# Grid attention: probabilities divided on VectorE ahead of their turn, in place of a spread of the reciprocals by transpositions

## What is computed

```python
def neighborhood_attn(q, k, v, rpb):
    ...
    def one(r):
        ...
        s = jnp.einsum('bqhd,bikhd->bhqik', qblk, kblk).astype(jnp.float32) * scale + bias
        s = jnp.where(colmask[:, None, :], s, -jnp.inf)
        p = jax.nn.softmax(s.reshape(B, H, GRID_W, kr * GRID_W), axis=-1)
        ...
        return jnp.einsum('bhqik,bikhd->bqhd', p, vblk)
...
            y = jnp.concatenate([yc, ym], axis=-1) * jax.nn.silu(gate)
            x = x + y @ w_out_odd[o]
```

## Time and profile before

| | |
|---|---|
| median of 3 runs | 2340.4 us (2339.95 to 2343.82) |
| profiled execution, time | 2340.63 us |
| profiled execution, span from first to last instruction | 2338.9 us |
| TensorE busy | 2257.0 us (96% of the span) |
| VectorE busy | 1584.3 us (68%) |
| ScalarE busy | 1305.0 us (56%) |
| GpSimd busy | 683.1 us (29%) |
| chain of work that ended last | TensorE 81%, VectorE 9%, ScalarE 4% |
| grid attention stage | about 1025 to 1545 us |

### The profile page before, as it was taken

The page is one execution under the profiler, slowest core; times in us unless marked ns, Lnnn a source line. Parts: engine busy times, 40 slices in busy tenths (PEclk is TensorE's granted clock), DMA queues, the critical chain, the costliest instruction groups (busy, mean ns, idle before and its releaser), DMA issues.

```text
span 2338.9 us, 35387 instructions
## 1 busy us (share of the span) xinstructions
PE 2257.0 (96%) x11778; PEld 1918.3 (82%) x11778; DVE 1584.3 (68%) x3262; ACT 1305.0 (56%) x3054; POOL 683.1 (29%) x843
## 2 busy tenths in 40 slices
PE   7999999999999999999999999899999999999999
PEld 6888888888888878888888888787787888887887
DVE  7444677677886433346655566658888878889787
ACT  6444566666775444446565566655656645465542
POOL 3455232311235642222222222565563200000000
PEclk9999999999999999999999999999999999999999
DMA  7322101111233342322322322633343633345734
GB/s 229 116 76 60 41 28 37 32 35 48 62 121 109 99 136 68 95 68 86 95 85 80 95 87 88 193 91 117 100 145 108 202 96 95 109 151 167 231 116 137
DMA packets 332356, 241.69 MB, mean 103 GB/s; under 512 B 66448, under 2 KB 284816, under 8 KB 331664
## 3 DMA queue, kind: packets, MB, share of 16 engines
q1 hardware_dynamic: 332176, 239.43, 33.6%
HBM read 195.59 MB, written 43.78 MB: 102 GB/s over the span
## 4 chain that ended last, share of the span: by engine, by line
PE 81%; DVE 9%; ACT 4%; issue 3%; DMA 1%; POOL 1%; SPq 1%; DVEq 0%; ACTq 0%; POOLq 0%
PE PS L1943 15%; PE PS L1945 15%; PE PS L1944 15%; PE PS L2176 6%; PE PS L2177 6%; PE PS L2178 6%; PE PS L2092 5%; PE PS L2059 5%; PE PS L2045 2%; PE PS L2046 2%; ACT PY L2187 1%; PE PS L2101 1%; PE PS L2000 1%; DVE ST L2555 1%; PE PS L2083 1%
## 5 line engine op out<-in xcount | busy, mean ns | idle before, releaser
L2852 POOL TENSOR_TENSOR WS<-WR,WS 128x256 fp32r<-128x256 f32 x635 | 493.4, 798 | 990.9 <-ACT WS L2187 990.1
L1943 PE MATMUL PS<-HT,WS 128*128 128x512 f32 x1492 | 602.5, 404 | 18.2 <-POOL WS L2852 6.2
L1945 PE MATMUL PS<-HT,WS 128*128 128x512 f32 x1492 | 584.0, 391 | 0.0
L1944 PE MATMUL PS<-HT,WS 128*128 128x512 f32 x1492 | 582.3, 390 | 0.0
L1943 PEld LDWEIGHTS PS<-HT,WS 128*128 128x128 f32 x1492 | 281.2, 188 | 76.6 <-issue 12.2
L1945 PEld LDWEIGHTS PS<-HT,WS 128*128 128x128 f32 x1492 | 280.7, 188 | 61.6
L1944 PEld LDWEIGHTS PS<-HT,WS 128*128 128x128 f32 x1492 | 281.7, 189 | 52.0
L2187 ACT ACTIVATE WS<-WR 128x256 fp32r<-128x256 f32 x658 | 245.3, 410 | 90.1 <-PE PS L1945 57.7
L2187 ACT ACTIVATE PT<-PS 128x512 fp32r<-128x512 f32 x352 | 186.2, 529 | 193.5 <-PE PS L2059 192.9
L2445 DVE TENSOR_TENSOR PT<-PS,PT 128x512 fp32r<-128x512 f32 x352 | 211.1, 609 | 84.5 <-ACT PT L2187 81.5
L2092 PE MATMUL PS<-PT,QKV 128*128 128x256 f32 (+3 forms) x1248 | 207.8, 288 | 3.5 <-DVE YB L2624 2.4
(11 more groups left out here) (284 smaller groups left out, 4554.9 us busy)
## 6 DMA issues: line engine op xcount, KB each, us to landing
WR<-in_w_in_odd SPq DMA_DIRECT2D x106, 256.0 KB, 2.9
EO<-in_grid SPq DMA_DIRECT2D x48, 384.0 KB, 3.1
WR<-in_ffn_in SPq DMA_DIRECT2D x60, 256.0 KB, 2.9
WR<-in_w_in_even SPq DMA_DIRECT2D x100, 128.0 KB, 2.5
WR<-in_w_out_odd SPq DMA_DIRECT2D x48, 256.0 KB, 2.8
yd<-PY SPq DMA_DIRECT2D x44, 256.0 KB, 3.3
EO<-in_ffn_in SPq DMA_DIRECT2D x35, 256.0 KB, 3.1
WR<-in_w_in_even SPq DMA_DIRECT2D x34, 256.0 KB, 2.9
```

Of the source, the lines that this page charges most:

```text
L1943: e.matmul(out, wh, rh, start=start, stop=False)
L1944: e.matmul(out, wh, rl, start=False, stop=False)
L1945: return e.matmul(out, wl, rh, start=False, stop=stop)
L2852: e.tensor_tensor(ws(i, 1, n), RAW[raw_slot(u)][:, o:o + n], f32(ws(i, 0, n)), ALU.subtract).then_inc(s_wlop.sem, 1)
```

## The change

For chunks of the kinds in `EARLY`, here grid attention alone, the softmax is divided before the turn. A new step "divide" multiplies each probability tile in `PY` by its column of reciprocals and by 0.5 on VectorE, in place. The reciprocals are made just before it, and the turn waits for it (`s_div`). The finish of such a chunk has no transpositions of `RW`, no copy into `RW`, and no multiplication of the gate by the spread reciprocals. In `stream`, the reciprocals and divisions of the waiting job are put ahead of the new job's scores; in `drain`, ahead of `begin_job`. Memory attention and the even layer are as before.

```diff
+EARLY = ("c",)
...
+        self.early = kind in EARLY
...
-        self.y = fin + (2 if c.mem else 4)
+        self.y = fin + (2 if c.mem else 4) - c.early
...
-            s.wide = s.x == 1 and s.h == 1
+            s.wide = s.x == 1 and s.h == 1 and not s.c.early
...
+        def divide(job):
+
+            for s in job.scores:
+                recip(s)
+            for s in job.scores:
+                s.divided = s_div.add()
+                put("divide", s)
...
-            f = Fin(c, pp, s_spread.add(), s_fin.n, s_yc.n, s_pv.n, c.rec[pp])
-            s_fin.add(2 if c.mem else 4)
+            f = Fin(c, pp, s_spread.n if c.early else s_spread.add(), s_fin.n, s_yc.n, s_pv.n, c.rec[pp])
+            s_fin.add(f.y - f.fin)
...
-            if job:
+            if job and not job.c.early:
                 for s in job.scores:
                     recip(s)
...
+            if job.c.early:
+                divide(job)
             begin_job(job)
...
                     job = pend["job"]
+                    if job and job.c.early:
+                        divide(job)
                     s0 = score(c, pp, h, 0)
...
                     w.wait_ge(s_exp, job.scores[1].no)
+                    if job.c.early:
+                        w.wait_ge(s_div, job.scores[1].divided)
                     w.wait_ge(*until[B_PT + pb])
...
                     f, = of
+                    if f.c.early:
+                        until[B_O] = (s_fin, f.y if f.c.mem else f.fin + 2)
+                        continue
                     w.wait_ge(s_rec, f.rec)
...
+                elif kind == "divide":
+                    s, = of
+                    p, rd = p_at(s.c, s.slot, 0, s.nk), RD[:, s.pp % 2, s.x, s.h:s.h + 1]
+                    w.wait_ge(s_rec, s.rec)
+                    e.tensor_scalar(p, p, rd, 0.5, ALU.mult, ALU.mult).then_inc(s_div.sem, 1)
...
-                    w.wait_ge(s_spread, f.no)
                     w.wait_ge(s_ed, max(c.gate) if c.grid else c.gate[f.pp // 2])
-                    e.scalar_tensor_tensor(out=sg, in0=spread, scalar=0.5, in1=sg, op0=ALU.mult, op1=ALU.mult).then_inc(s_fin.sem, 1)
+                    if not c.early:
+                        w.wait_ge(s_spread, f.no)
+                        e.scalar_tensor_tensor(out=sg, in0=spread, scalar=0.5, in1=sg, op0=ALU.mult, op1=ALU.mult).then_inc(s_fin.sem, 1)
```

More of the change, by code:

```diff
@@ L345, in build @@
         s_mm, s_ea, s_ed, s_flip, s_rs, s_rp = (signal(n) for n in ("s_mm", "s_ea", "s_ed", "s_flip", "s_rs", "s_rp"))
-        s_score, s_mx, s_exp, s_sink, s_rec = (signal(n) for n in ("s_score", "s_mx", "s_exp", "s_sink", "s_rec"))
+        s_score, s_mx, s_exp, s_sink, s_rec, s_div = (signal(n) for n in ("s_score", "s_mx", "s_exp", "s_sink", "s_rec", "s_div"))
         s_turn, s_pth, s_ptl, s_pv = (signal(n) for n in ("s_turn", "s_pth", "s_ptl", "s_pv"))
@@ L2613, in vector_program @@
                             w.wait_ge(sig, value)
-                    w.wait_ge(s_spread, f.no)
                     w.wait_ge(s_ed, max(c.gate) if c.grid else c.gate[f.pp // 2])
-                    e.scalar_tensor_tensor(out=sg, in0=spread, scalar=0.5, in1=sg, op0=ALU.mult, op1=ALU.mult).then_inc(s_fin.sem, 1)
+                    if not c.early:
+                        w.wait_ge(s_spread, f.no)
+                        e.scalar_tensor_tensor(out=sg, in0=spread, scalar=0.5, in1=sg, op0=ALU.mult, op1=ALU.mult).then_inc(s_fin.sem, 1)
                     if c.mem:
                         w.wait_ge(s_pv, f.pv)
-                        w.wait_ge(s_fin, f.fin + 1)
+                        w.wait_ge(s_fin, f.y - 1)
                         e.tensor_tensor(y, PS[:, B_O, 0:256], sg, ALU.mult).then_inc(s_fin.sem, 1)
@@ L2624, in vector_program @@
                         e.tensor_tensor(YB[HALF[x], :], YB[HALF[x], :], PS[HALF[x], B_O, 256 * x:256 * x + 256], ALU.add).then_inc(s_fin.sem, 1)
-                    w.wait_ge(s_fin, f.fin + 3)
+                    w.wait_ge(s_fin, f.y - 1)
                     e.tensor_tensor(y, yb, sg, ALU.mult).then_inc(s_fin.sem, 1)
```

## The result

The changed kernel takes 2502.7 us in the median of four runs (2497.2 to 2505.7), against 2342.1 for the kernel before, measured beside it. The ratio is 1.0683, with a 95% interval of 1.0660 to 1.0707: 6.8% slower. The forecast was 2487 us (6% more), with 2440 to 2535 as the range.

The account below looks back on a forecast made before the run. TensorE was taken to bound the grid stage. From 2340.6 us, less 7.7 for transpositions, plus 124 of waits and 30 of lower clock, the forecast was 2487 us, range 2440 to 2535.

Parts of the forecast that it names:

- What bounds the kernel, and the place: Grid stage: TensorE bounds, busy 508.41 of 520 us; VectorE's multiplications behind the projection's low halves delay the turn.
- The transpositions, -7.7 us: Grid finishes on TensorE: 64 transpositions go, worth 0.12 us each from start to start, 7.7 us less.
- The price behind the table add's old start, 1.0 us: Each grid job: two reciprocals, two multiplications and hand-over make probabilities ready 1.0 us after the table add's old start.
- The waits, 124 us net: TensorE's turns in the grid stage: waits for VectorE recur in every job and add up to 124 us.
- The clock, 30 us: TensorE in the grid stage: 19 falls to half clock after waits, 1.6 us each, 30 us.
- Outside the stage, nothing: Ahead of and behind the grid stage: nothing changes except the place of what follows.
- Rival 1: Grid stage: waits come but the clock holds, or waits are partly swallowed; 2457 down to 2435 us; chance 0.20.
- Rival 2: Grid stage: half clock follows nearly every wait, 75 us; 2532 us, or 2549 with dearer multiplications; chance 0.15.
- Rival 3: Grid turns: multiplications are ready before the turn, only the transpositions' time is left; 2333 us; chance 0.03.
- Rival 4: Grid blocks: only each block's first wait counts as other engines get ahead, 30 to 60 us; 2365 to 2400; chance 0.06.

Follow-up runs that it names:

- the filled kernel: Changed kernel with 848 transpositions of the identity run on TensorE ahead of the turn's wait: 2456.0 us, ratio 1.0495.
- the early place: Changed kernel with reciprocals and multiplications moved right behind the job's exponentials, ahead of the projection's low parts in VectorE's list: 2340.7 us, ratio 0.9989.

## Why the prediction was right

**What bounds the kernel, and the place.** Right, and it carried the forecast: the waits are where VectorE's list had put the low parts in front.

**The transpositions, -7.7 us.** Right. The 64 of the memory attention brought 7.5 us, 0.12 each, from start to start; by their records' length they would have brought 18.

**The price behind the table add's old start, 1.0 us.** Right. The turn of the first job is 4.33 us late from start to start, which is 3.33 plus 1.0, and the seven waits of a regular block make 18.3 us where I had 18.1. It is the sum of the small terms that was right: two reciprocals take 0.20 us to the first multiplication (I had 0.25), the two multiplications 0.65 us (0.59), the hand-over 0.15 (0.14). The copy's price was the right one to go by: 96 more columns cost a multiplication that runs alone some 0.05 us, and the table add 0.10.

**The waits, 124 us net.** Nearly right. Gross I had 133, and the terms of that sum make 51 jobs; the 47 that stand beside it in the prediction are a miscount. The trace has 51 waits, 123.7 us by their rows and 131.8 from start to start. Of the gaps that the kernel before has in this stage 9.7 us are gone, where I had taken off 9. Net that is 122 us. What misses is the last block: 17.2 us gross, where I had counted 20.3.

**The clock, 30 us.** The place was right, the size a little too small. The stage grew by 148.1 us; with 7.7 gone and 122 of waiting that leaves 34 us for slow matmuls, and the filled kernel gives 36. I had 19 falls of 3.4 us. The trace has 20 places in the stage, but in nine of them the clock stayed low for 6.8 us, so there are 29 stretches of 3.4. All 13 waits over 3 us were followed by a fall, and seven of the other 38 waits. Against that a stretch cost less than the 1.6 us I had given it, 1.2 to 1.3 us (34 to 36 us over the 28 that are new). So two misses stand against each other in this term: the count of stretches too low, the price of one too high. That it came out near is in part luck. Windows of the changed kernel show both kinds: the first is a short one, the other two lie in one long stretch.

```profile
1131.00:1135.00 4.00, 4.00 (x17) 3.42 (x16) 1.90 (x6) 2.46 (x7) 0.73 (x1) 0.57 0.00 0
...
1374.00:1377.00 3.00, 2.18 (x11) 2.17 (x12) 2.27 (x10) 0.94 (x2) 0.00 (x0) 0.50 0.04 8
1377.00:1380.00 3.00, 3.00 (x9) 2.32 (x8) 1.92 (x5) 2.43 (x9) 0.73 (x1) 0.50 0.41 129
```

**Outside the stage, nothing.** Here I missed a term: 8.4 us (3.0 ahead and 5.4 behind), with the same instructions in the same order. The clock was low in eleven stretches of 3.4 us there, against three before and a part of one in the last 2.6 us. As nothing outside the stage was changed, I put it down to which of the gaps that both kernels have are followed by a fall, and this differs from run to run. The other traces bear that out. The same instructions ahead of the stage and behind it took, with the number of low stretches in brackets (one that the end cuts off counts as a part): 1822.6 us before (3.8), 1821.9 with the reciprocals moved (4.0), 1822.7 with the multiplications doubled (3.8), 1823.2 at the early place (5.0), 1824.1 there with work that nobody waits for (3.6) and 1825.6 with the low parts on VectorE (9.0), 1826.7 in the filled kernel (8.0), 1830.9 in the changed kernel (11.0). These kernels have one trace each. But the two that wait most, the changed one and the one with the doubled multiplications, are 8.2 us apart, which speaks for the execution and against the change; and it has the size of the differences between the changed kernel's own runs (2497.2 to 2505.7). Why the same gap is followed by a fall in one execution and not in another is open.

The sum of the profiled execution: -7.7 + 122 + 34 + 8.4, which is the 156.5 us up to rounding; the 34 are what the others leave, so that it adds up is no test. The test is the filled kernel's 36. Against the forecast the waits were 2 us too high, the clock 4 to 6 and the outside 8 too low.

**The rivals.** Rival 1, waits without a clock term, is nearly what the filled kernel shows (2456, where I had worked out 2457); the changed kernel itself is not it. Rival 2 was wrong: 20 of 51 waits were followed by a fall and not nearly all, and its 75 us were 34 to 36. Rival 3 came true only for the early place, where it gave 2341 and not 2333: its condition was read right for most jobs, but eight turns still wait, and the clock fell for longer beside two of them. Part of it is what GpSimd does to a multiplication at that time. Rival 4 is refuted by the doubled multiplications.

## What to carry to other kernels

Where all engines walk through one list, a step that another engine waits for must be put by what stands in front of it on its own engine, not by how long it takes: here some 50 us of VectorE's work cost 160 us behind the projection's low parts, and ahead of them the kernel came out 1.3 us faster than before. The price of such a wait is the distance in the timeline between the two engines at that place, times the number of passes, and it doesn't shrink from pass to pass if the work in front waits for the waiting engine's own last instruction. To read such a wait from a profile take it from start to start: the idle time in a row leaves out what the records overlap, here 8 us over 51 waits. Add to it what the clock takes from TensorE when it stands, and look whether GpSimd works at the place where VectorE's instruction is to go.

## What the runs showed of the hardware

- TensorE's clock went to 0.50 (1.2 GHz) during or within 3 us behind every one of 13 waits of 4 us and more, and seven of 38 of 1.0 to 2.6 us; in nine of 20 places it stayed there for 6.8 us and not for 3.4. Such a stretch of 3.4 us cost 1.2 to 1.3 us of time.
- The same instructions, those outside the grid stage, had between 3.6 and 11 such stretches in the traces of eight kernels, and took 1821.9 to 1830.9 us.
- TensorE given transpositions of the identity to do while it waits kept its clock at 1.00 through the stage: one stretch of 3.4 us is left of 29. The Trainium skill (TensorE: Matmul & The Clock Gate, Part 4: PE-mode transpose) says that the full clock does not engage for transpositions; the trace of the filled kernel doesn't agree, at least for these float32 ones between matmuls. Whether transpositions alone would hold the clock up no run here shows.
- An in-place multiplication of 128x384 by a column takes 0.41 us and of 128x288 0.37 when GpSimd stands. Beside GpSimd's subtractions of weights (128x256) it takes up to 0.96 us, and beside one of 128x512 up to 1.46.
